# Two-layer encoder trunk on one core: score passes over 128 rows instead of 64, and tiles on 64-byte places

## What is computed

```python
def stick_window_mixer(h, w_in, sinks, w_out):
    proj = h @ w_in                                # sq sk sv wq wk wv
    o_sb = stick_breaking_attention(...)           # 8 heads of 64
    o_sw = sliding_window_sink_attention(...)      # 8 query heads, 2 key heads of 64
    o = jnp.concatenate([o_sb, o_sw], axis=-1)
    return o @ w_out

# stick-breaking, per block of 128 queries
    z = jnp.einsum('bhqd,bshd->bhqs', qblk, kf)
    log_keep = jnp.where(strict, jax.nn.log_sigmoid(-z), 0.0)
    later = lax.cumsum(log_keep, axis=3, reverse=True) - log_keep
    wts = jnp.where(strict, jnp.exp(jax.nn.log_sigmoid(z) + later), 0.0)
    out = jnp.einsum('bhqs,bshd->bqhd', wts, vf)

# band heads
    logits = jnp.einsum('bnqkgd,bnskd->bnkgqs', qb, kb) + bias   # ALiBi, window of two chunks
    p = jnp.exp(logits - m); denom = sum(p) + exp(sink - m)
    out = jnp.einsum('bnkgqs,bnskd->bnqkgd', p / denom, vb)

# feed-forward
    return (jax.nn.gelu(conv(h @ w_gate)) * (h @ w_up)) @ w_down
```

## Time and profile before

| | |
|---|---|
| median of three executions | 1421.26 us |
| profiled execution, its own time | 1426.75 us |
| its span, first to last instruction | 1424.8 us |
| PE busy | 1355.5 us, 95% |
| PE weight loads (beside passes) | 1089.2 us, 76% |
| DVE busy | 800.0 us, 56% |
| ACT busy | 552.4 us, 39% |
| POOL busy | 49.6 us, 3% |
| mean granted clock of PE | 0.968 |
| instructions | 17254 |

### The profile page before, as it was taken

One profiled execution on the slowest core, in us unless ns is written; L12 is line 12 of the kernel. 1 busy time (PEld: TensorE's weight loads), 2 busy tenths in 40 slices (PEclk: granted clock), 3 DMA queues, 4 the chain that ended last, 5 costly groups with the idle time before them and its releaser, 6 DMA issues.

```text
span 1424.8 us, 17254 instructions
## 1 busy us (share of the span) xinstructions
PE 1355.5 (95%) x6208; PEld 1089.2 (76%) x6208; DVE 800.0 (56%) x1170; ACT 552.4 (39%) x827; POOL 49.6 (3%) x95
## 2 busy tenths in 40 slices
PE   4899997888999999999998999999999999999998
PEld 3676764676788888887877888888778888888785
DVE  6453435646756665644577777775765555452323
ACT  5444453423433333312135555553353333332212
POOL 1000000000000000000110000000000000000000
PEclk7799998999999999999999999999999999999999
DMA  9333333014354445454732222222523333322232
GB/s 363 101 99 93 100 93 104 1 59 148 106 151 140 147 144 151 133 175 136 246 124 74 75 65 71 74 74 89 163 74 95 97 99 92 103 88 102 76 103 74
DMA packets 189266, 160.35 MB, mean 113 GB/s; under 512 B 4959, under 2 KB 164920, under 8 KB 189218
## 3 DMA queue, kind: packets, MB, share of 16 engines
q1 hardware_dynamic: 177008, 116.41, 26.7%
q0 software_dynamic: 11936, 43.14, 9.5%
q10 hardware_dynamic: 274, 0.16, 0.0%
HBM read 157.59 MB, written 2.10 MB: 112 GB/s over the span
## 4 chain that ended last, share of the span: by engine, by line
PE 90%; DVE 4%; ACT 3%; DMA 1%; SPq 1%; issue 1%; DVEq 0%; ACTq 0%
PE proj L1342 60%; PE z L1342 23%; PE obank L1342 3%; PE misc L1342 2%; DMA w_raw<-ab_w_in 1%; SPq L426 1%; ACT w_hi L546 1%; DVE w_lo L866 1%; DVE soft L1009 0%; PE z L1502 0%; PE z L1762 0%; ACT q_sb L633 0%; DVE xT L1169 0%; PE z L1740 0%; ACT soft_a L633 0%
## 5 line engine op out<-in xcount | busy, mean ns | idle before, releaser
L1342 PE MATMUL proj<-hT_hi,w_hi 128*128 128x512 f32 x1168 | 470.1, 403 | 19.1 <-DVE hT_lo L894 7.1
L866 DVE TENSOR_TENSOR w_lo<-w_raw,w_hi 128x1024 fp32r<-128x1024 f32 x198 | 242.4, 1225 | 400.5 <-ACT w_hi L546 400.5
L1342 PE MATMUL proj<-hT_lo,w_hi 128*128 128x512 f32 x1168 | 460.5, 394 | 0.0
L1342 PE MATMUL proj<-hT_hi,w_lo 128*128 128x512 f32 x1168 | 460.1, 394 | 0.0
L546 ACT ACTIVATE w_hi<-w_raw 128x1024 fp32r<-128x1024 f32 x198 | 209.6, 1059 | 512.7 <-PE proj L1342 322.9
L1342 PEld LDWEIGHTS proj<-hT_hi,w_hi 128*128 128x128 f32 x1168 | 222.7, 191 | 73.8 <-issue 20.7
L1342 PEld LDWEIGHTS proj<-hT_hi,w_lo 128*128 128x128 f32 x1168 | 222.8, 191 | 47.9
L1342 PEld LDWEIGHTS proj<-hT_lo,w_hi 128*128 128x128 f32 x1168 | 223.3, 191 | 45.1 <-issue 1.7
L1342 PE MATMUL z<-gated_hi,w_hi 128*128 (+1 forms) x352 | 141.2, 401 | 2.6 <-DVE xT L1169 2.6
L1342 PE MATMUL z<-gated_lo,w_hi 128*128 (+1 forms) x352 | 139.2, 395 | 0.0
L1342 PE MATMUL z<-gated_hi,w_lo 128*128 (+1 forms) x352 | 139.2, 395 | 0.0
(11 more groups left out here) (224 smaller groups left out, 1327.6 us busy)
## 6 DMA issues: line engine op xcount, KB each, us to landing
ada_raw<-ada_w POOLq DMA_DIRECT2D x80, 512.0 KB, 4.1
w_raw<-ffn_w_gate SPq DMA_DIRECT2D x44, 512.0 KB, 3.7
w_raw<-ffn_w_up SPq DMA_DIRECT2D x44, 512.0 KB, 3.8
w_raw<-ffn_w_down SPq DMA_DIRECT2D x44, 512.0 KB, 3.7
w_raw<-hg_w_in SPq DMA_DIRECT2D x32, 512.0 KB, 4.0
w_raw<-ab_w_in SPq DMA_DIRECT2D x18, 512.0 KB, 4.0
ada_first<-ada_w SPq DMA_DIRECT2D x7, 1024.0 KB, 17.1
w_raw<-ab_w_out SPq DMA_DIRECT2D x8, 512.0 KB, 4.1
```

The source lines that it names most:

```text
L866: nc.vector.tensor_tensor(w_lo[:, slot, :], w_raw[:, slot, :], w_hi[:, slot, :].bitcast(F32), ALU.subtract).then_inc(lo_done, 1)
L1342: return nc.tensor.matmul(dst, weights_ap, moving, start=start, stop=stop, skip_group_check=True)
```

## The change

- **Keys of the stick-breaking heads.** The even head's keys stay in k_sb, whose rows 64 to 127 are zero; the odd head's keys go to rows 64 to 127 of another tile whose rows 0 to 63 are zero. These four tiles (`k_odd`) are tiles that lie unused during layer 0's mixer: the halves of h32 and of square. The score pass multiplies 128 rows of keys by 128 rows of q_sb; the other head's queries meet zeros.
- **Queries of the band heads.** In the same way, even heads in q_sw and odd heads in `q_odd` (both parts of normed, sumsq and rstd), against all 128 rows of k_sw.
- **Zeros.** DVE clears eight half tiles for the keys ahead of its first step of STEPS0, and eight for the queries at step B of head 0, after the band keys are copied. ACT waits for k_clear, DVE for q_clear (8) before the writes.
- **Writes.** ACT writes a key tile in two pieces of 64 rows, DVE a query tile in two.
- **Places.** normed gets 2 x 528 numbers for 2 x 514, sinks 16 for 8, and last_dec goes behind oT_lo. With these every tile starts on a multiple of 64 bytes but for a few of 96 bytes and less (lower). Before, gated_hi, gated_lo, table, table_r, ident_r, slope_r and most tiles of layer 1 up to key_nat started 32 bytes off; hT_hi, hT_lo, w_hi, w_lo, q_sb, k_sb, q_sw, k_sw, softplus, oT_hi and oT_lo did not.

```diff
+LINE = 16
-        normed = sb("normed", [P, 2, SEQ + 2])
+        normed = sb("normed", [P, 2, SEQ + LINE])
-            sinks = sb("sinks", [P, SW_HEADS], F32, s0)
+            sinks = sb("sinks", [P, LINE], F32, s0)
-            last_dec = sb("last_dec", [P, 2, TB], F32, s1)
             masks = sb("masks", [P, P + LEVELS * 2 * P], F32, s1)
             oT1 = sb("oT1", [P, 2, SEQ], F32, s1)
             oT_hi = sb("oT_hi", [P, DC, SEQ], F32R, s1)
             oT_lo = sb("oT_lo", [P, DC, SEQ], F32R, s1)
+            last_dec = sb("last_dec", [P, 2, TB], F32, s1)
+        k_odd = [h32[:, 0, :], h32[:, 1, :], square[:, 0, :], square[:, 1, :]]
+        q_odd = [normed[:, 0, LINE:LINE + SEQ], normed[:, 1, LINE:LINE + SEQ], sumsq[:], rstd[:]]
+        def sb_keys(b):
+            return k_odd[b // 2] if b % 2 else k_sb[:, b // 2, :]
+        def sw_queries(h):
+            return q_odd[h // 2] if h % 2 else q_sw[:, h // 2, :]
...
                         elif SK <= b:
-                            nc.scalar.activation(k_sb[:, b - SK, :], proj[u % 2][:], ACT.Copy
+                            act.wait_ge(k_clear, 2 * (b - SK) + 2)
+                            nc.scalar.activation(k_sb[0:HEAD, b - SK, :], proj[u % 2][0:HEAD, :], ACT.Copy)
+                            nc.scalar.activation(k_odd[b - SK][HEAD:P, :], proj[u % 2][HEAD:P, :], ACT.Copy
                                                  ).then_inc(proj_free[u % 2], 1)
...
+            for hp in range(4):
+                nc.vector.memset(k_sb[HEAD:P, hp, :], 0.0).then_inc(k_clear, 1)
+                nc.vector.memset(k_odd[hp][0:HEAD, :], 0.0).then_inc(k_clear, 1)
+            def clear_queries():
+                for hp in range(4):
+                    nc.vector.memset(q_sw[HEAD:P, hp, :], 0.0).then_inc(q_clear, 1)
+                    nc.vector.memset(q_odd[hp][0:HEAD, :], 0.0).then_inc(q_clear, 1)
...
-                            nc.vector.tensor_scalar(q_sw[:, b - WQ, :], src[:], HEAD ** -0.5, None, ALU.mult
-                                                    ).then_inc(proj_free[u % 2], 1)
+                            hp = b - WQ
+                            dve.wait_ge(q_clear, 8)
+                            nc.vector.tensor_scalar(q_sw[0:HEAD, hp, :], src[0:HEAD, :], HEAD ** -0.5, None,
+                                                    ALU.mult)
+                            nc.vector.tensor_scalar(q_odd[hp][HEAD:P, :], src[HEAD:P, :], HEAD ** -0.5, None,
+                                                    ALU.mult).then_inc(proj_free[u % 2], 1)
...
+                elif kind == "B" and b == 0:
+                    clear_queries()
...
-                    last = mm(z[:, lo:lo + n], q_sw[r, hp, b * P:(b + 1) * P],
-                              k_sw[r, g, (b + 1) * P - n:(b + 1) * P], stop=True)
+                    last = mm(z[:, lo:lo + n], sw_queries(h)[:, b * P:(b + 1) * P],
+                              k_sw[:, g, (b + 1) * P - n:(b + 1) * P], stop=True)
...
-                        mm(zb[j][:, 0:Z_LEN[j]], k_sb[r, hp, j * P:(j + 1) * P], q_sb[r, hp, j * P:SEQ],
+                        mm(zb[j][:, 0:Z_LEN[j]], sb_keys(b)[:, j * P:(j + 1) * P], q_sb[:, hp, j * P:SEQ],
                            start=True)
```

More of the change, by code:

```diff
@@ L326, in trunk @@
         pt_dve = sem("pt_dve")
+        k_clear = sem("k_clear")
+        q_clear = sem("q_clear")
         hv_ready = sem("hv_ready")
@@ L511, in _ @@
             pool.dma_start(table2, tables[:, 2 * P:9 * P]).then_inc(const_in, 16)
-            pool.dma_start(sinks[:], ab_sinks.partition_broadcast(P).rearrange("p a h -> p (a h)")
+            pool.dma_start(sinks[:, 0:SW_HEADS], ab_sinks.partition_broadcast(P).rearrange("p a h -> p (a h)")
                            ).then_inc(const_in, 16)
@@ L1477, in window_logits @@
                 s, hp, g = h % 3, h // 2, h // SW_GROUP
-                r = slice(HEAD * (h % 2), HEAD * (h % 2) + HEAD)
                 tile_in(WQ + hp)
@@ L1541, in _ @@
                 elif kind == "A":
-                    hp, r = b // 2, slice(HEAD * (b % 2), HEAD * (b % 2) + HEAD)
+                    hp = b // 2
                     tile_in(SQ + hp)
```

## The result

The changed kernel takes 1401.9 us (median of four executions, 1401.33 to 1405.01), the kernel before 1422.15 in the executions beside it: ratio 0.9858, 95% interval 0.9839 to 0.9877. The forecast was 1395.3, with a range of 1388 to 1405: the direction and the range held, but of the 26.0 us forecast some 20 came. The profiled execution of the changed kernel took 1405.01 us (before 1426.75), its span is 1403.2 (before 1424.8), so the two traces differ by 21.6.

What follows compares the result with a forecast made beforehand. The prediction took TensorE (PE) to bound the kernel, with 90% of the chain that ended last. Its terms, -10.0 - 6.8 - 2.2 - 7.0 = -26.0 us, gave 1395.3 us against the 1421.26 median, range 1388 to 1405.

Steps and rivals of the forecast that it cites:

- Term 1: Stick-breaking heads: score blocks of twelve 128-row passes, without shape changes, drop from 3.86 to 2.65 us; -10.0 us.
- rival that rows do not matter: Score blocks are slow because fp32 and fp32r alternate; terms 1 to 3 go, 1414.3 us; chance 0.04.
- Term 2: PE clock behind score blocks of heads 0, 1 and 6: the half-clock stretches vanish; -6.8 us, other end 0.
- Term 3: Band heads: logits blocks drop from 2.72 to 2.00 us, gaining only for heads 1 to 3; -2.2 us.
- Term 4: Down projections: gated put on a multiple of 64 bytes, each pass 0.0066 us shorter; -7.0 us, other end 0.
- rival that the down projections keep their pace: The 0.0066 us is of the bank or weights, not the address; 1402.3 us; chance 0.14.
- Term 5: Added clears and writes on DVE and ACT fit into idle time; 0 us.
- the clock still falling: Rival: PE's clock still falls behind score blocks, since their passes stay at a low rate; 1402.1 us; chance 0.14.
- The slower rival: Zero rows make the clock fall oftener, behind all eight score blocks and in the band heads; 1432 us; chance 0.04.

Runs made afterwards that it cites:

- masks_behind: Kernel before, 64-row passes kept, with the four mask passes of a score block gathered behind its eight score passes: 1411.41 us, one execution.
- places_only: Kernel before with only the changed places of normed, sinks and last_dec, 64-row score passes kept: 1422.75 us, ratio 0.9988.
- zeros_only: Changed kernel without its new places, so only the 128-row tiles with zeros: 1405.55 us, ratio 0.9888.
- place_128: Changed kernel with gaps of 48 numbers ahead of gated in both layers and ahead of oT: 1404.59 us, ratio 0.9877.
- line128: Changed kernel with cond and lower padded so that all tiles behind them stand on multiples of 128 bytes: 1408.55 us, ratio 0.9896.
- place_sweep: Changed kernel with gaps of 56 and 32 numbers ahead of gated (layers 0, 1) and 8 ahead of oT: 1412.21 us, one execution.
- clears_early: Changed kernel with the key-tile clears moved: h32 and square ahead of DVE's first split, k_sb's as one behind the last hT_lo: 1402.05 us, ratio 0.9844.
- after_again: Changed kernel run again without any edit, on another chip: 1403.97 us, ratio 0.9859 to the kernel before.

## Why the prediction was right in direction and 6.6 us too low

- **Term 1, score blocks, -10.0: right.** Eight blocks at full clock took 3.87, 31.0 in all, and take 20.95 now: 2.55 behind a unit, 2.66 behind a value block (forecast 2.65). A unit's last pass ahead of three of them went from 0.318 to 0.227, another 0.3, as forecast: -10.3 in all. masks_behind bears out the reason, change of shape, over the rival that rows do not matter: that rival has its premise right (64 rows in one shape cost what 128 do) and its consequence wrong, since the slow part was never the rows; and the alternation of fp32 and fp32r, to which it put the cost, is still there in blocks of 2.66 us.
- **Term 2, the clock behind score blocks, -6.8: right where it was placed, not as a sum.** No fall from 64 to 207 us in any of the kernels with 128-row blocks, nor in masks_behind; places_only keeps three. From the first score block to that of head 7 it is 157.0 us before and 141.8 after: -15.2, where seven blocks and this term made -15.6. What failed is that the term took the falls of one trace as all there is to the clock. In the profiled execution the falls near 712 and 736 us are 6.8 us longer together, and layer 1's mixer grew by 2.1 us. That is no price of the faster score blocks: zeros_only has these and no long fall there (its layer 1 mixer takes 239.79 us for 240.87), and places_only has the long falls with the old blocks.
- **Term 3, band heads, -2.2: nearly right, and the clock on top.** The logits block of head 3 takes 2.03 (238.50 to 240.52) for 2.71. The chain through heads 1 and 2 (in order of time, changed kernel) answers to the earlier trace rows:

```profile
228.91 2.14 PE z L1372 x10
231.14 0.44 DVE soft L1033
...
234.78 1.09 DVE soft_a L1044 x4
...
238.57 2.13 PE proj L1372 x10
```

  DVE's maxima now begin behind the first head's block, where before they began behind both. Ahead of DVE's normalisation the chain now goes through ACT's exponentials (1.56 us from 232.59), which the working did not have on the path. (Its "6.7" runs to 252.21, DVE's first step behind the maxima; to the 252.52 that it names it is 7.0.) From the first logits pass of heads 1 and 2 to the transposes of head 1 it is 7.1 us (228.84 to 235.91) for 8.2: -1.1, where -1.5 was forecast, and head 3's block gives the -0.7. The stretch from the first transposes (224.05, before 240.29) to the end of head 3's block (240.52, before 261.04) is nevertheless 4.3 us shorter, since the kernel before had the clock at half in PE's transposes and value blocks there (237.59 to 244.41 and 251.24 to 258.07 us), the changed one only up to 227.39. The 2.5 us over the -1.8 I put down to the clock, at a place where I had forecast none; no run tries it by itself. Heads 4 to 7 keep their two heads in 11.41 us, 5.7 each, as ACT sets them:

```profile
250.02 0.17 DVE L1040 TENSOR_TENSOR soft<-soft 128x4 f32<-128x4 f32 x1 [0.89 <-ACT soft L648]
...
261.43 0.16 DVE L1040 TENSOR_TENSOR soft<-soft 128x4 f32<-128x4 f32 x1 [0.89 <-ACT soft L648]
```

- **Term 4, addresses, -7.0: the step that failed, by its cause and by its size.** The working read off two numbers, 0.2333 over gated and 0.2267 over oT, and gave a reason that fitted: 33 pieces of 64 bytes for 32. The numbers were right; the reason was a coincidence of size, and place_128, line128 and place_sweep leave nothing of it: no run shows such pieces. On its 64-byte place gated runs at 229.2 ns, not 226.7, and the down projections gained 3.8 us (256.6 to 252.7), not 7.0. The pace follows the distance to the weights within 256 bytes; at distance zero the 0.2267 is there (place_128), and 1056 x (233.2 - 227.0) ns would be 6.5 us. The change even took oT from distance 0 to +64: 192 passes at 229.1 for 227.5, +0.3. The fast tiles, hT and oT, share two things, a multiple of 64 bytes and the distance to the weights; the working named the first and did not see the second. The rival that the down projections keep their pace was wrong too: they got half of what the term gave them.
- **Term 5, added work, 0: slightly wrong.** The clears were counted at 0.485 without the 0.16 us of issue behind each, 3.9 for 5.1, against a cover of 4.94. The w_lo of 56.96 came at 57.30, 0.17 of it since the whole start was later, and PE waited. By clears_early and the distance of the second unit this is 0.1 us in the profiled execution and up to 1.4 in others. The clears of the query tiles, also 5 us, did stay covered, as did the added writes: no new wait of PE from 64 to 200 us.

Summed over the profiled executions: score blocks and the three falls -15.2 up to head 7 and -1.2 behind it, band heads -4.2, down projections -3.8; a start 0.2 later (the first pass over hT at 44.02 for 43.85, and 0.1 by the clears, less 0.1 of the last pass ahead of the first score block); the rest +2.6, of which layer 1's mixer has 2.1 and the slower oT 0.3; together -21.6. Against the forecast 3.2 us are missing from term 4 and 2.6 are lost where it had nothing; 2.0 more than forecast came from the band heads. The median, 1401.9, lies where the forecast had put two of its rivals (1402.3 with the old pace of the down projections, 1402.1 with the clock still falling), and neither happened: that the numbers meet is chance. The range held since its upper end left room for a miss of this size. Its lower end does not follow from the working: 1395.3 less 1.9 for the mask passes and 1.75 for the band heads is 1391.6, not 1388.

The slower rival had nothing: with rows of zeros the clock fell nowhere from 64 to 212 us, in ten traces, and the band heads ran at 0.94 for 0.89.

## What to carry to other kernels

Before padding an operand to full rows, look whether passes of different shapes alternate: gathering the passes of one shape got 1.0 of the 1.2 us of a block back here, with no added work and no tiles of zeros. When a row shows two paces for the same pass, list everything that the fast cases share (here also the distance between the two operands) before naming a cause, and move one thing at a time. Compare the whole list of stretches at half clock before and after: here three that were understood went, and two elsewhere doubled, with nothing changed there but, as far as the traces tell, the moment at which they began. So price a change worth 2 to 4 us by the pace of its own passes at full clock, and not by the median of the whole alone. And count issue gaps when work is put into an engine's idle time.

## What the runs showed of the hardware that was not expected

- A pass of 512 columns of fp32r takes 226.9 to 233.4 ns by where the streamed tile lies from the weights within 256 bytes, 3% between best and worst, in all kernels run; w_hi and w_lo moved by 128 bytes brought the passes over hT from 227 to 232.5.
- A change of shape between 64 and 128 contracted rows costs 0.15 to 0.17 us in a score block; eight of them made a block of 2.66 us one of 3.86. To alternate fp32 and fp32r in one shape costs nothing that shows (0.97 us for three passes either way).
- The clock fell behind six of sixteen blocks with eight changes of shape (before, places_only), though PE showed no idle time, and behind none with two or none, in the eleven traces of kernels with such blocks (ten with 128 rows, and masks_behind). Which heads trip differs from kernel to kernel.
- Falls at the start of a stage last 3.4 or 6.8 us by the moment at which they begin against its first pass: at layer 0's feed-forward 0.51 us ahead still gave 3.4 (the changed kernel), 0.52 ahead 6.8 (place_128), with the same passes over the same tiles. That is how the traces sort; it was not tried by itself. Such falls are part of why place_128 stood 81.5 us at half clock for 68.8 in after_again (medians), and why its faster passes do not show in its median.
- A clear of 64x512 numbers takes 0.48 us on DVE and 0.16 to the next; one of 64x2048 takes 1.76, for the 2.4 of four in a row: 0.7 us cheaper.
